# A mixture-of-experts stage with five weight sets, and its down product in 32-row blocks on four column tiles

## The chip, the cores and the metric

The kernel runs on one core of a Trainium2 chip. The metric is the device time of one execution in microseconds (us), lower is better. Before the change it is 932.44 us, the median of three runs (931.26 to 933.4).

## The reference, cut to what matters

One streaming step of a one-layer encoder for 512 prompt tokens and 64 sample tokens (576 in all, width 1024, fp32): a combined projection, an SSD and an S5 mixer, cross-attention over 256 memory rows, a two-level mixture of experts, and a final norm. The change is in the experts. Each token takes two of 32 experts, and every expert's weights are read, 3 MiB for each:

```python
for e in range(N_EXPERTS):                                       # 32
    hid = jax.nn.silu(t @ p["w_gate"][e]) * (t @ p["w_up"][e])   # (T,1024) @ (1024,256), twice
    out = out + (hid @ p["w_down"][e]) * combine[:, e:e + 1]     # (T,256) @ (256,1024)
```

## The kernel before, in words

The kernel is written out by hand, engine by engine, with semaphores. The dense part (projections, mixers, attention) runs until the routing is known. It streams its weights through a ring of six 1 MiB slots. After it comes the expert stage, which is this case.

**One expert.** Routing gives each expert a list of up to 80 rows (`CAP`). For expert n, GpSimd (POOL) issues an indirect DMA that gathers the rows from DRAM (`gather`, L802, into `xg[b]`). TensorE turns them in eight transposes (`turn_x`, recorded under L865, into banks 0 and 1). ScalarE and VectorE copy the turned rows to `xgT[b]` (L1695, L2244). TensorE computes gate and up (L1375: 64 fp32 matmuls of 80 columns on two column tiles of 64; the trace shows each fp32 matmul as two instructions, each with a weight load, so 128). ScalarE takes the silu (L1700), and VectorE multiplies (recorded under L1755, into `hid[b]`). TensorE computes down (L1387: four fp32 matmuls, 80 rows by 512 columns, eight instructions in the trace). ScalarE and VectorE copy one half each to `yo[b]` (L1707, L2257), and POOL scatters the rows to DRAM with a second indirect DMA (`scatter`, L817).

**Buffers.** `xg`, `xgT`, `gact`, `hid`, `yo` and the banks of down (4 and 5, or 6 and 7) exist twice; b is the parity of n, so experts take them in turn.

**Order on TensorE.** gate/up of n, transposes of n+1, down of n, gate/up of n+1. The transposes lie between gate/up and down, so that silu and product run meanwhile. **Order on POOL.** scatter of n, gather of n+3. A gather waits until the expert that used its `xg` buffer last has been turned. A scatter, and the copies to `yo` before it, wait until the last scatter from the same buffer has landed.

**Weights.** Four sets of three 1 MiB parts (gate, up, down), `WSET`. SyncE (SP) loads expert n+4 into the set of n: gate and up when gate/up of n is done, down when down of n is done (`load_part`, recorded under L654). The first four sets are loaded during the last of the dense part, each part when its memory is free (`WFREE`). TensorE's loop has four experts in its body, the loops of the other engines two; the first and last experts are written out. `pass` loops for more than 80 rows per expert exist and are skipped here.

L991 is another product of the dense part: a weight block of 8 columns against 128 columns, with its four token tiles at output partitions 0, 32, 64 and 96, that is on four column tiles, 64 instructions in rounds of four.

Of the kernel before, what the change touches and what calls it, by code (L numbers as in the profile page):

```python
# [12 lines left out]
ACT = mybir.ActivationFunctionType  # L13
# [6 lines left out]
D = 1024  # L20
# [19 lines left out]
CW = 256  # L40
# [5 lines left out]
CAP = 80  # L46
PASSES = -(-T // CAP)
SKIP = float(1 << 12)
# [172 lines left out]
def build(nc, a, o):  # L221
# [14 lines left out]
    with ExitStack() as ctx:  # L236
# [179 lines left out]
        more_loaded = [sem(f"more_loaded{i}") for i in range(6)]  # L416
# [44 lines left out]
        xg_zero, experts_done = sem("gather_buffers_zeroed"), sem("experts_done")  # L461

# [40 lines left out]
        def wait_chunk(eng, c):  # L503
# [12 lines left out]
        LAST = NE // 2 - 1  # L516
# [5 lines left out]
        WSET = [ring_k[0:3], ring_k[3:6], [g0, g1, a0], [a1, b0, b1]]  # L522
        WSEM = [ring_loaded[0:3], ring_loaded[3:6], more_loaded[0:3], more_loaded[3:6]]
        SETS = len(WSET)
        QUADS = NE // SETS

        WFREE = ([chunk_end[max(c for c in range(NCH) if c % SLOTS == k)] for k in range(SLOTS)]
                 + [("pv", 2 * NT - 1)] * 2 + [("route", NT - 1)] * 2 + [("o", NT - 1, 1)] * 2)
        WDENSE = [len(range(i, NCH, SLOTS)) for i in range(SLOTS)] + [0] * 6
# [4 lines left out]
        def wait_expert_chunk(eng, part, qq, s):  # L534

            eng.wait_ge(WSEM[s][part], 16 * qq + 16 * (WDENSE[3 * s + part] + 1))

# [14 lines left out]
        def _(sp):  # L552
# [91 lines left out]
            def load_part(qq, i, s, part):  # L644

                if isinstance(qq, int) and qq == 0:
                    wait_filled(sp, *WFREE[3 * s + part])
                    if s == 2:
                        sp.wait_ge(kv_stored, 32)
                elif part < 2:  # L650
                    sp.wait_ge(gu_done, 4 * qq + (s - 3))
                else:
                    sp.wait_ge(dn_done, 8 * qq + (2 * s - 6))
                sp.dma_start(WSET[s][part], experts_of[part][bass.ds(SETS * i + s, 1), :, :]  # L654
                             .rearrange("e p n -> p (e n)")).then_inc(WSEM[s][part], 16)

            def sp_pass(p):
                first = p * QUADS

                order = [(0, 0), (1, 2), (2, 0), (2, 1), (0, 1), (0, 2), (1, 0), (1, 1), (2, 2), (3, 0), (3, 1), (3, 2)]  # L660
                for s, part in (order if isinstance(p, int) else sorted(order)):
                    load_part(first, 0, s, part)
# [1693 lines left out]
```

## Time and profile before

| what | value |
|---|---|
| median of three runs | 932.44 us (931.26 to 933.4) |
| the profiled execution | 939.89 us, its span 938.1 us |
| TensorE busy | 857.6 us (91% of the span) |
| mean granted TensorE clock | 0.96 of 2.4 GHz |
| expert stage: first gate/up to last down | 598.1 to 899.8 us of the span |
| memory traffic | 166.5 MB, of which 100.7 MB are expert weights |

The span runs from the first instruction to the last; the profiled execution adds 1.8 us around it. Engines are PE (TensorE matmul), PEld (its weight loads), DVE (VectorE), ACT (ScalarE), POOL (GpSimd) and SP (SyncE, which only issues DMAs). "L1387" is a line of the kernel. Matmuls are pipelined, so a row's mean duration is longer than the distance from one to the next; the distance is what counts in a sum.

### The profile page before, as it was taken

To read this page: it belongs to the slowest core of one execution; us is meant where nothing else is said; L and a number is where in the kernel's file an instruction comes from. 1 tells how busy PE (TensorE), PEld (TensorE's weight loads), DVE (VectorE), ACT (ScalarE), POOL (GpSimd) and SP (SyncE) were. 2 spreads that over 40 slices of the span, in tenths; PEclk is the share of its full clock that TensorE was granted. 3 is DMA by queue.
4 is the path that set the end of the run, shared out by engine and by line. 5 is a ranking of instruction groups with operands and counts; after the bars stand their busy time and mean duration, and the time that the engine had idled before them with its cause. 6 is when DMAs were issued, how large, how long until landed. Compare 5 with 4: busy or idle time off the path is not lost. (4 is left out here: it accounts for less than half of the span.)

```text
span 938.1 us, 18956 instructions
## 1 busy us (share of the span) xinstructions
PE 857.6 (91%) x7993; PEld 679.9 (72%) x7993; DVE 354.7 (38%) x767; ACT 195.4 (21%) x435; POOL 144.3 (15%) x175
## 2 busy tenths in 40 slices
PE   3999999889999999999999996799999999999930
PEld 2778877777888888877888885676767676767620
DVE  5599896524551123401223448211111111111117
ACT  2312307325221101112221211111111111111104
POOL 1190100003420000000000000121212222222103
PEclk9999999989999999999999997699999999999975
DMA  9630073202121840241020036599999999999435
GB/s 247 206 98 1 10 176 106 74 13 93 46 90 68 292 169 1 70 155 45 1 90 23 23 113 258 195 346 351 360 350 356 361 361 375 370 364 369 147 139 187
DMA packets 71418, 166.48 MB, mean 177 GB/s; under 512 B 20592, under 2 KB 51440, under 8 KB 58496
## 3 DMA queue, kind: packets, MB, share of 16 engines
q1 hardware_dynamic: 58500, 150.86, 45.5%
q0 software_dynamic: 6144, 9.45, 3.0%
q10 hardware_dynamic: 6716, 5.34, 1.8%
q8 instruction: 43, 0.70, 0.3%
q14 instruction: 15, 0.12, 0.0%
HBM read 158.09 MB, written 17.88 MB: 188 GB/s over the span
## 5 line engine op out<-in xcount | busy, mean ns | idle before, releaser
L898 PE MATMUL bank<-act_a,weight_ring 128*128 128x288 f32 x768 | 190.5, 409 | 1.8 <-ACT act_a L1427 1.8
L898 PEld LDWEIGHTS bank<-act_a,weight_ring 128*128 128x128 f32 x768 | 146.1, 191 | 42.0 <-ACT act_a L1427 2.4
L1206 PE MATMUL bank<-weight_ring,act_b 128*128 128x256 f32 x512 | 111.8, 379 | 0.0
L1206 PEld LDWEIGHTS bank<-weight_ring,act_b 128*128 128x128 f32 x512 | 96.7, 190 | 12.9
L1375 PEld LDWEIGHTS bank<-region_t,weight_ring 128*64 128x64 f32 x2048 | 75.4, 142 | 12.9 <-issue 12.0
L1375 PE MATMUL bank<-region_t,weight_ring 128*64 128x80 f32 x2048 | 77.9, 238 | 0.7 <-ACT region_t L1695 0.7
L1755 DVE TENSOR_TENSOR region_t<-region_t,bank 128x160 f32<-128x160 f32 (+3 forms) x47 | 15.6, 331 | 145.7 <-PE bank L1375 145.3
L817 POOL DMA_INDIRECT expert_rows<-region_r,scatter_now x32 | 30.1, 940 | 207.2 <-DVE region_r L2257 207.2
L2257 DVE COPY region_r<-bank 80x512 f32<-80x512 f32 x32 | 22.0, 687 | 103.9 <-PE bank L1387 103.9
L1387 PE MATMUL bank<-weight_ring,region_t 128*80 128x512 f32 x128 | 58.2, 597 | 1.5 <-DVE region_t L1755 1.0
L1110 PE MATMUL bank<-weight_ring,region_u 128*128 128x256 f32 x256 | 58.3, 388 | 0.0
L1110 PEld LDWEIGHTS bank<-weight_ring,region_u 128*128 128x128 f32 x256 | 49.5, 194 | 7.1
L865 PE MATMUL bank<-ident,region_r 80*128 80x80 f32 (+2 forms) x328 | 45.2, 281 | 3.9 <-DMA region_r<-ffn_rows,gather_index 3.9
L1427 ACT ACTIVATE act_a<-bank 128x512 f32<-128x512 f32 (+1 forms) x46 | 22.5, 523 | 120.4 <-PE bank L865 91.5
L1755 DVE TENSOR_TENSOR region_u<-region_u,bank 128x512 f32<-128x512 f32 (+1 forms) x20 | 13.7, 687 | 85.0 <-PE bank L1206 81.5
L865 PEld LDWEIGHTS bank<-ident,region_r 80*128 80x128 f32 (+2 forms) x328 | 39.2, 190 | 8.5 <-issue 4.5
L785 POOL MEMSET region_r<- 80x1024 f32 x2 | 1.8, 948 | 267.8 <-PE bank L1266 267.8
L1375 PEld LDWEIGHTS bank<-region_t,region_g 128*64 128x64 f32 x1024 | 36.5, 138 | 6.4 <-issue 6.4
L865 PE MATMUL bank<-ident,row_stage 128*128 128x128 f32 (+3 forms) x173 | 23.1, 283 | 18.7 <-DVE row_stage L1773 16.8
L1387 PEld LDWEIGHTS bank<-weight_ring,region_t 128*80 128x80 f32 x128 | 17.9, 150 | 29.9 <-issue 29.4
L1375 PE MATMUL bank<-region_t,region_g 128*64 128x80 f32 x1024 | 37.8, 234 | 0.0
L1700 ACT ACTIVATE region_t<-bank 128x160 f32<-128x160 f32 x32 | 9.7, 303 | 133.2 <-PE bank L1375 133.2
(332 smaller groups left out, 1107.3 us busy)
## 6 DMA issues: line engine op xcount, KB each, us to landing
weight_ring<-in_w_gate SPq DMA_DIRECT2D x16, 1024.0 KB
weight_ring<-in_w_down SPq DMA_DIRECT2D x16, 1024.0 KB
weight_ring<-in_w_up SPq DMA_DIRECT2D x16, 1024.0 KB
weight_ring<-in_w_in SPq DMA_DIRECT2D x8, 1024.0 KB
region_g<-in_w_gate SPq DMA_DIRECT2D x8, 1024.0 KB
region_g<-in_w_up SPq DMA_DIRECT2D x8, 1024.0 KB
act_a<-in_w_down SPq DMA_DIRECT2D x8, 1024.0 KB
act_a<-in_w_gate SPq DMA_DIRECT2D x8, 1024.0 KB
```

The costliest lines, as they stand in the source:

```text
L785: pool.memset(xg[b][0:CAP], 0.0).then_inc(xg_zero, 1)
L817: pool.indirect_dma_start(out=y2_dram[:, :], out_offset=bass.IndirectOffsetOnAxis(ap=cur_y[0:CAP, b:b + 1], axis=0), in_=yo[b][0:CAP], in_ ...
L865: return pe.transpose(out, in_, ident[0:m, 0:m])
L898: m = pe.matmul(ps[:, 0:HALF], slot(c)[:, k, P * (mt % 2):P * (mt % 2 + 1)], x[:, k, HALF * h:HALF * (h + 1)], start=(k == 0), stop=(k == ...
L1110: m = pe.matmul(ps[:, 0:CW], mnT[:, k, P * t:P * (t + 1)], slot(first_chunk + c)[:, k, :], start=(k == 0), stop=(k == KD - 1))
L1206: m = pe.matmul(ps[0:L, CW * cc:CW * (cc + 1)], x[:, k, t0:t0 + L], slot(c)[:, k, :], start=(k == 0), stop=(k == KD - 1))
L1375: m = pe.matmul(banks[2 + part][cols, CAP * j:CAP * (j + 1)], w[:, k, j::2][:, cols], xgT[b][:, k, :], start=(k == 0), stop=(k == KD - 1))
L1387: m = pe.matmul(banks[4 + 2 * b + h][0:CAP, :], hid[b][:, j, :], down[:, D * j + 512 * h:D * j + 512 * (h + 1)], start=(j == 0), stop=(j = ...
L1427: act.activation(dst, src, func, scale=scale).then_inc(emptied["act"], 1)
L1700: act.activation(gact[b].rearrange("p j l -> p (j l)"), banks[2][:, 0:2 * CAP], ACT.Silu)\
L1755: return dve.tensor_tensor(out, x, y, op)
L2257: dve.tensor_copy(yo[b][0:CAP, 512:D], banks[5 + 2 * b][0:CAP, :]).then_inc(yo_dve, 1)
```

## The change

Three things are changed together.

1. **Five weight sets.** `SETS = 5`; the three extra parts lie in memory that the dense part has left by then (`conv_io`, the upper half of `region_t`), and all parts are grouped anew by the time at which their memory is free. Fifteen loads are issued ahead (`PREFETCH`); SP loads expert n+5 into the set of n.
2. **Down in blocks.** The 80 rows are cut into blocks of 32, 32 and 16, the 1024 columns into quarters of 256. The twelve (block, quarter) pairs run in three rounds of four, each round on the four column tiles: blocks 0, 1, 2 of quarter r, and block r of quarter 3. An expert's down is 24 fp32 matmuls of 256 columns. ScalarE makes three copies from the banks where it made one, VectorE two where it made one.
3. **Loops of five.** All engines write out seven experts and then loop five times over five. The double buffers follow `side(n) = n % 5 % 2`: 0, 1, 0, 1, 0, and again 0, 1, 0, 1, 0. The experts 4 and 5, 9 and 10, and so on to 29 and 30 take the same buffer in direct succession (six pairs).

The order of the steps on TensorE is unchanged, and so is POOL's order (scatter n, gather n+3). The core of the diff:

```diff
+DB = 32
+SETS = 5
+PEEL = 2 + SETS
+ROUNDS = (NE - PEEL) // SETS
...
+        def down_block(b, blk, quarter):
+            p0 = DB * 3 if quarter == 3 else DB * blk
+            spot = blk if quarter == 3 else quarter
+            n_ = min(CAP, DB * (blk + 1)) - DB * blk
+            return banks[4 + 2 * b + spot // 2][p0:p0 + n_, CW * (spot % 2):CW * (spot % 2 + 1)]
...
-        WSET = [ring_k[0:3], ring_k[3:6], [g0, g1, a0], [a1, b0, b1]]
+        c0, c1, t1 = view(conv, 0, 2048), view(conv, 2048, 2048), view(reg_t, 2048, 2048)
+        WSET = [[t1, ring_k[5], ring_k[0]], [c0, g0, c1], [g1, ring_k[1], ring_k[2]],
+                [ring_k[3], ring_k[4], b0], [b1, a0, a1]]
+        PREFETCH = [(0, 1), (0, 2), (1, 1), (2, 0), (0, 0), (1, 0), (1, 2), (2, 1), (2, 2), (3, 0), (3, 1), (3, 2),
+                    (4, 0), (4, 1), (4, 2)]
...
+        def side(n):
+            return n % SETS % 2
...
+        def wait_rows_free(eng, n, i, p):
+            done = times_used(n, i, p) - 1
+            if not isinstance(done, int) or done > 0:
+                eng.wait_ge(scattered[side(n)], 16 * done)
...
+            def reload(p, i, n):                                   # SyncE
+                N = NE * p + SETS * i + n
+                for part in range(3):
+                    if part < 2:
+                        sp.wait_ge(gu_done, N - (SETS - 1))
+                    else:
+                        sp.wait_ge(dn_done, 2 * N - 2 * (SETS - 1))
+                    load_part(SETS * i + n, n % SETS, part)
...
+            def gather(n, i, p, reused=True):                      # GpSimd
+                b = side(n)
                 if reused:
-                    pool.wait_ge(turned_x, 4 * pp + (2 * b - 2))
+                    before_it = max(m for m in range(-SETS, n) if side(m) == b)
+                    pool.wait_ge(turned_x, 2 * NE * p + 2 * SETS * i + 2 * (before_it + 1))
...
-                for h in range(2):                                 # TensorE, down
-                    for j in range(2):
-                        m = pe.matmul(banks[4 + 2 * b + h][0:CAP, :], hid[b][:, j, :],
-                                      down[:, D * j + 512 * h:D * j + 512 * (h + 1)], start=(j == 0), stop=(j == 1))
-                    m.then_inc(dn_done, 1)
+                for r in range(3):
+                    for j in range(2):
+                        for blk, quarter in [(0, r), (1, r), (2, r), (r, 3)]:
+                            m = pe.matmul(down_block(b, blk, quarter), hid[b][:, j, DB * blk:min(CAP, DB * (blk + 1))],
+                                          down[:, D * j + CW * quarter:D * j + CW * (quarter + 1)],
+                                          start=(j == 0), stop=(j == 1))
+                    if r > 0:
+                        m.then_inc(dn_done, 1)
...
+                with pe.Fori(0, ROUNDS) as i:
+                    for n in range(PEEL, PEEL + SETS):
+                        turn_x(n, i, p)
+                        down_rows(n - 1, i, p)
+                        gate_up(n, i, p)
+                down_rows(NE - 1, 0, p)
...
+                wait_rows_free(act, n, i, p)                       # ScalarE
+                for blk in range(2):
+                    act.activation(yo[b][DB * blk:DB * (blk + 1), 3 * CW:D], down_block(b, blk, 3), ACT.Copy)
                 act.activation(yo[b][0:CAP, 0:512], banks[4 + 2 * b][0:CAP, :], ACT.Copy).then_inc(yo_act, 1)
...
-                dve.tensor_copy(yo[b][0:CAP, 512:D], banks[5 + 2 * b][0:CAP, :]).then_inc(yo_dve, 1)
+                dve.tensor_copy(yo[b][DB * 2:CAP, 3 * CW:D], down_block(b, 2, 3))
+                dve.tensor_copy(yo[b][0:CAP, 2 * CW:3 * CW], banks[5 + 2 * b][0:CAP, 0:CW]).then_inc(yo_dve, 1)
```

## Rows read from the trace of the kernel before

**Rows 1.** The page: busy time by engine, then 40 slices of the span.

```profile
PE 857.6 (91%) x7993; PEld 679.9 (72%) x7993; DVE 354.7 (38%) x767; ACT 195.4 (21%) x435; POOL 144.3 (15%) x175
...
PEclk9999999989999999999999997699999999999975
DMA  9630073202121840241020036599999999999435
```

**Rows 2.** Busy time in one window of the expert stage.

```profile
core 0: us, PE busy (x) PEld busy (x) DVE busy (x) ACT busy (x) POOL busy (x), PEclk, DMA share, GB/s
672.00:866.00 194.00, 192.45 (x2967) 136.49 (x2967) 30.69 (x61) 27.24 (x61) 47.25 (x82) 1.00 0.98 363
```

**Rows 3.** Waits of TensorE, 620 to 900 us, its only row: sum, times, longest.

```profile
PE bank L1387 <- DVE region_t L1755: 1.5, 6, 0.5
```

**Rows 4.** Timeline, one expert of the steady stretch, weight loads left out.

```profile
703.54 0.69 DVE L2257 COPY region_r<-bank 80x512 f32<-80x512 f32 x1 [3.33 <-PE bank L1387]
705.21 0.94 POOL L817 DMA_INDIRECT expert_rows<-region_r,scatter_now  x1 [6.35 <-DVE region_r L2257]
...
707.21 0.98 POOL L802 DMA_INDIRECT region_r<-ffn_rows,gather_now  x1 [0.86 <-POOL gather_now L796]
...
707.92 1.11 PE L865 MATMUL bank<-ident,region_r 80*128 80x80 f32 x8
...
709.05 3.66 PE L1387 MATMUL bank<-act_b,region_t 128*80 128x512 f32 x8
...
711.03 0.59 ACT L1707 ACTIVATE region_r<-bank 80x512 f32<-80x512 f32 x1 [1.93 <-PE bank L1387]
...
712.64 4.83 PE L1375 MATMUL bank<-region_t,weight_ring 128*64 128x80 f32 x128
...
717.41 1.11 PE L865 MATMUL bank<-ident,region_r 80*128 80x80 f32 x8
...
718.12 0.44 ACT L1695 ACTIVATE region_t<-bank 128x320 f32<-128x320 f32 x1 [1.96 <-PE bank L865]
```

**Rows 5.** Matmul groups by form: count, then busy us, mean ns, idle before.

```profile
L1387 PE MATMUL bank<-weight_ring,region_t 128*80 128x512 f32 x128 | 58.2, 597 | 1.5 <-DVE region_t L1755 1.0
...
L991 PE MATMUL bank<-act_a,w_dt 128*8 128x128 f32 x64 | 2.1, 273 | 0.0
```

**Rows 6.** Timeline, the first expert and the first reused gather.

```profile
591.99 1.20 POOL L802 DMA_INDIRECT region_r<-ffn_rows,gather_index  x1 [44.45 <-issue]
...
596.12 1.30 PE L865 MATMUL bank<-ident,region_r 80*128 80x80 f32 x8 [3.89 <-DMA region_r<-ffn_rows,gather_index]
...
597.60 0.18 POOL L796 COPY gather_now<-gather_index 80x1 int32<-80x1 int32 x1 [3.15 <-PE bank L865]
...
598.12 6.96 PE L1375 MATMUL bank<-region_t,weight_ring 128*64 128x80 f32 x128 [0.70 <-ACT region_t L1695]
598.65 0.97 POOL L802 DMA_INDIRECT region_r<-ffn_rows,gather_now  x1 [0.87 <-POOL gather_now L796]
```

**Rows 7.** Timeline of SyncE, first reload of a weight set.

```profile
605.26 0.35 SPq L654 DMA_DIRECT2D weight_ring<-in_w_gate  x1
```

**Rows 8.** The scatter line, the whole run: issue to landing.

```profile
DMA to landing us min/median/max: 3.3/7.5/7.8
```

**Rows 9.** DMA queue of gathers and scatters, 672 to 866 us: packets, MB, share.

```profile
q0 software_dynamic: 3940, 6.59, 9.8%
```

**Rows 10.** The page: the queue that fetches instructions, whole run.

```profile
q8 instruction: 43, 0.70, 0.3%
```

**Rows 11.** Windows around a short lull of TensorE: busy, clock (PEclk).

```profile
200.00:203.60 3.60, 1.89 (x16) 1.50 (x15) 2.40 (x4) 1.96 (x3) 0.00 (x0) 1.00 0.25 73
203.00:207.00 4.00, 4.00 (x11) 2.89 (x10) 0.00 (x0) 0.41 (x1) 0.00 (x0) 0.58 0.00 0
```

**Rows 12.** Timeline of TensorE there.

```profile
200.82 0.70 PE L865 MATMUL bank<-ident,region_u 72*128 72x72 f32 x8 [0.60 <-ACT region_u L1427]
202.63 5.57 PE L1048 MATMUL bank<-act_b,weight_ring 128*128 128x288 f32 x15 [1.12 <-DVE act_b L1758]
```

More of the change, by code:

```diff
@@ L657, in sp_pass, with load_part @@
[L657 to L662, printed above, removed]
-                with sp.Fori(1, QUADS) as i:
+            def load_part(e, s, part):
+                sp.dma_start(WSET[s][part], experts_of[part][bass.ds(e, 1), :, :]
+                             .rearrange("e p n -> p (e n)")).then_inc(WSEM[s][part], 16)
@@ L664, in sp_pass @@
                     for s in range(SETS):
                         for part in range(3):
-                            load_part(first + i, i, s, part)
+                            load_part(s, s, part)
+                whole = NE // SETS - 1
+                with sp.Fori(0, whole) as i:
+                    for s in range(SETS):
+                        reload(p, i, SETS + s)
+                for n in range(SETS * (whole + 1), NE):
+                    reload(p, 0, n)
             sp_pass(0)
@@ L1707, in act_expert @@
                 act.activation(yo[b][0:CAP, 0:512], banks[4 + 2 * b][0:CAP, :], ACT.Copy).then_inc(yo_act, 1)
             def act_pass(p):
-                first = p * (LAST + 1)
-                again = not isinstance(p, int)
-                copy_x(first, 0)
-                for b in range(2):
-                    act_expert(first, b, reused=again)
-                with act.Fori(1, LAST) as i:
-                    for b in range(2):
-                        act_expert(first + i, b)
-                for b in range(2):
-                    act_expert(first + LAST, b, last=(b == 1))
+                copy_x(0, 0, p)
@@ L1721, in _ @@
+                act_gate(0, 0, p)
+                for n in range(1, PEEL):
+                    copy_x(n, 0, p)
+                    act_rows(n - 1, 0, p)
+                    act_gate(n, 0, p)
+                with act.Fori(0, ROUNDS) as i:
+                    for n in range(PEEL, PEEL + SETS):
+                        copy_x(n, i, p)
+                        act_rows(n - 1, i, p)
+                        act_gate(n, i, p)
+                act_rows(NE - 1, 0, p)
             act_pass(0)
@@ L2300, in dve_pass @@
                     expert_gates()
[L2301 to L2308 removed]
+                copy_x(0, 0, p)
+                dve_hidden(0, 0, p)
+                for n in range(1, PEEL):
+                    copy_x(n, 0, p)
+                    dve_rows(n - 1, 0, p)
+                    dve_hidden(n, 0, p)
+                with dve.Fori(0, ROUNDS) as i:
+                    for n in range(PEEL, PEEL + SETS):
+                        copy_x(n, i, p)
+                        dve_rows(n - 1, i, p)
+                        dve_hidden(n, i, p)
+                dve_rows(NE - 1, 0, p)
             dve_pass(0)
```

195 lines of the change are left out of this document (94 added, 101 removed).

## The prediction

> **What bounds the kernel now.** I read the page first, then windows, the waits of TensorE, the timeline of one expert, and the DMA queues. TensorE is busy 91% of the span [rows 1]. In the last third, the expert stage, two digits stand side by side: from the 27th slice to the 37th the TensorE clock and the DMA row both show 9 in every slice. So both could be the bound. The window from 672 to 866 us tells them apart: TensorE is busy 192.45 of 194 us, the DMA engines 98%, at 363 GB/s [rows 2]. An expert has 144 matmul instructions (128 for gate/up, 8 transposes, 8 for down), so 2967 of them are 20.6 experts, one per 9.42 us. If the weights were late, TensorE would show idle time ahead of L1375. Its only waits from 620 to 900 us are 1.5 us, and on VectorE's product [rows 3]. TensorE sets the pace, and the DMA engines stand just beside the limit.
>
> The timeline shows what the 9.42 us are: transposes 707.92 to 709.05 (1.13), down 709.05 to 712.64 (3.59), gate/up 712.64 to 717.41 (4.77 here; 4.70 is what the mean leaves) [rows 4]. Whatever TensorE sheds per expert counts 32 times, until something else is late. Behind it stand the gather, whose rows are turned next, and the weights.
>
> **Down in blocks.** Before: eight instructions of 512 columns, 58.2 us for 128 [rows 5], so near 0.43 us from one to the next by the length of L1387 in the timeline; 8 x 0.43 = 3.44, and 3.59 to the next line's start leaves 0.15 of hand-over. A pass is thus 0.84 ns per column. After: 48 instructions of 256 columns, 0.215 us each. One after the other they would take 10.3 us, so all hangs on four running at once. L991 is the trace's own case of four column tiles with all 128 rows: 64 instructions of 128 columns, 0.107 us each, 6.8 us in a row, yet 2.1 us busy [rows 5]. Less the last one's 0.27, that is 0.122 us for each round of four. The upper bound for down is 12 rounds x 0.215 x 0.122 / 0.107 = 2.94 plus 0.15, so 3.09 us; the lower 12 x 0.215 + 0.15 = 2.73. I take 2.75, near the lower end, as the excess of L991 is partly its start and would weigh half as much on rounds twice as long. The saving is 0.84 us per expert (bounds 0.50 to 0.86), x 32 = **26.9 us** (16 to 27.5).
>
> The Trainium skill, page "TensorE: Matmul & The Clock Gate", section "Measured speedup vs the span model", gives 2.38 times for three column tiles, 79% of full overlap. By it a down would be 2.58 / 0.79 + 0.15 = 3.4 us and the saving 6 us in all. L991 shows at least 88%, and by it the sum above stands.
>
> The copies: ScalarE needs 0.44 us for 320 columns and 0.59 for 512 [rows 4], so 0.39 for 256; two more make 0.8 us, and it may start at two thirds of down. VectorE's 0.69 becomes two copies, about 0.85. Both lie beside gate/up of the next expert (4.7 us); the scatter is issued 0.2 us later. Cost on the path: 0.
>
> **The fifth set.** Per expert the DMA engines move 3.15 MB of weights and 6.59 / 20.6 = 0.32 MB of rows [rows 9]; at 363 GB/s that is 9.55 us, more than TensorE's new pace of 8.6. They would fall behind by about 1 us per expert, and prefetch pays for it. The first reload goes out at 605.26 [rows 7]. After the change 27 experts are still to come: 605 + 27 x 9.55 = 863 us, with latency 867. TensorE wants the last set, by the sum below, at about 884 (598.1 + 2.3 of cold clock + 31 x 9.42 - 26 + 18). Hidden with 17 us to spare; cost and gain 0. Were no stall to come, it would want it at 866, so the weights would cap the gain at about 25. The three more loads ahead fall in the dense part, where the DMA row has slices of 0 and 2 [rows 1]; SP's two added waits are for stores long done, and behind them SP has only these loads.
>
> **Loops of five, uneven turn.** This is the step that costs. Let expert 4 and 5 share a buffer. The gather of 5 may go only when 4 has been turned; before, it went when 3 had been. Queued behind that wait on POOL are the scatter of 3 and the gather of 6, both with time to spare. From the end of the transposes of 4: POOL reacts after 0.18 (597.42 to 597.60), copies its index and issues after 1.05 (598.65) [rows 6], the gather lands, 0.1 to TensorE. Meanwhile TensorE does down of 3 and gate/up of 4, 2.75 + 4.70 = 7.45 us, and stands. How long a gather takes no row says. From below, the first one is 591.99 to 596.12, 4.1 us, on quieter queues [rows 6]. From above, the one of 707.21 had landed without a wait at 717.41, 10.2 us [rows 4]. The nearest row is the scatter of the same 80 rows: 7.5 us median, 7.8 at most [rows 8]. I take 8.0. Then each stall is 0.18 + 1.05 + 8.0 + 0.1 - 7.45 = 1.9 us, and six pairs make **+11.4 us**.
>
> A second wait hangs on the same pair: the copies to `yo` of expert 5 wait for the scatter of 4. From the end of down of 4: copies and scatter issue 0.1 + 0.85 + 0.98 = 1.9 (0.98 as from 704.23, the copy's end, to 705.21 [rows 4]), landed at 9.5. Down of 5 ends at 8.6, so its copies end at 10.9, its scatter goes at 11.9, the gather of 8 at 13.9, landed 21.9; TensorE wants it at 21.9. Regularly it lands 1.3 us early. I price it 0.3 us at five places, **+1.5**.
>
> The clock: a stall and the transposes after it are 3 us in which TensorE does next to nothing. The trace has a like place: idle 0.60 and 1.12 around 0.70 of transposes [rows 12], and then a clock of 0.58 in the window of 203 to 207 [rows 11], that is some 3.4 us at 1.2 GHz, half of them lost, 1.7 us. It is the only such place that I lean on, so I charge three of the six stalls: **+5.1** (0 to 10).
>
> **Sum.** -26.9 + 11.4 + 1.5 + 5.1 = -8.9 us, on the profiled execution 939.9 to 931.0. The median of the runs lies 7.5 us below that execution; the difference is in neither term, so I predict 932.44 - 8.9 = **923.5 us**.
>
> **The rivals.**
> (a) The uneven turn costs nothing: if a gather lands in 6.1 us or less it is hidden. For: the lower bound of 4.1. Against: the scatters' 7.5. Time: -25, 907.
> (b) The loop does not stay in the instruction memory. TensorE's loop body grows from 4 x 288 to 5 x 368 = 1840 matmuls and loads. The 43 instruction fetches took 0.3% of 16 engines' 938 us, 1.05 us each [rows 10]; gathers and scatters slow down by 7.5 / 3.3 = 2.3 beside the weights [rows 8], so a backward jump that must fetch costs 1.05 to 2.4. Four jumps: +4.2 to +9.6, 928 to 933. For: nothing in the trace had so long a body. Against: 1152 fetched nothing visible. The Trainium skill, page "Runtime: NRT & Kernel Launch", section "Instruction fetch mechanics", gives TensorE 2048 instructions in blocks of 256 and warns of a taken branch to a block not held. By that page's figure 1840 and the waits fit only barely; no run here shows it yet.
> (c) Slower: gathers take longer than before because TensorE's faster pace fills the DMA engines wholly. Each us on a gather costs 6 for the pairs and 5 for the ripples, 11 us, so it decides from 8.0 + 8.9 / 11 = 8.8 us. At 9.5 it is 940, at the bound of 10.2 about 948. For: the share is 0.98 already. Against: it was 0.98 when scatters took 7.5.
> (d) The four blocks overlap only in part: down 3.1 to 3.4 us, saving 6 to 16, stalls 1.3 to 1.6 each, clock +5: 930 to 939.
>
> **How the numbers follow.** The forecast has 0.50, its own range 916 to 930. (a) 0.13, (b) 0.14, (c) 0.14, (d) 0.09. A change under 0.2% (930.6 to 934.3) is about what a measurement of this kernel can't tell from none. Faster: 0.49 + 0.13 + 0.06 of (b) + 0.02 = 0.70. Same: 0.01 + 0.06 of (b) + 0.02 of (c) + 0.03 of (d) = 0.12. Slower: 0.18. The range 911 to 937 leaves out most of (a) and the upper part of (c), 0.2 together.
>
> **What would show it.** Down: distance from its first instruction to the next line's, 2.75 us. Stalls: TensorE idle ahead of L865's transposes of experts 5, 10, ..., 30, released by a gather, near 1.9 us, none of that size elsewhere; PEclk below 1 after some. (b): idle of TensorE's queue after experts 11, 16, 21, 26. Weights: no idle ahead of the gate matmuls. I am wrong if down is over 3.1 us, if stalls of the pairs are under 1 or over 2.7 us, or if TensorE waits at other experts.

## The result and the profile after

The changed kernel takes 965.62 us (median of 4 runs, 963.13 to 968.57), the kernel before, beside it on the same chip, 931.85 us (4 runs, 931.17 to 933.4). The ratio is 1.0365, 95% interval 1.0342 to 1.0389: 33.8 us slower. The forecast was 923.5 us, with a range up to 937. The profiled execution of after took 963.13 us, with a span of 961.3 us. The expert stage runs from 599.9 to 923.3 us, 323.4 us; it was 301.7 us in the profiled execution of before.

The page of after: TensorE's busy time, the clock and DMA rows in 40 slices, and the queue that fetches instructions.

```profile
PE 845.2 (88%) x9273; PEld 695.6 (72%) x9273; DVE 359.8 (37%) x799; ACT 219.5 (23%) x499; POOL 144.1 (15%) x175
...
PEclk9999999989999999999999995999989999898975
DMA  9630073102212920510111528799989979898135
...
q8 instruction: 82, 1.34, 0.6%
```

Two things stand out against [rows 1] and [rows 10]. The DMA row no longer shows 9 in every slice of the stage, so the memory side isn't full: both former bounds now have slack at the same time. And the instruction queue brought 82 blocks where it had brought 43. Next, the window of [rows 2] in after, then the waits of TensorE in the stretch of [rows 3] (sum, times, longest).

```profile
672.00:866.00 194.00, 164.34 (x3331) 128.96 (x3324) 29.92 (x72) 37.96 (x91) 41.50 (x72) 0.92 0.89 325
```

```profile
PE bank L915 <- issue: 19.7, 4, 5.5
PE bank L915 <- DMA region_r<-ffn_rows,gather_now: 10.1, 5, 3.5
PE bank L1426 <- issue: 8.1, 8, 1.7
```

"issue" is time in which TensorE waited for nothing that the profile shows. Four such waits, near 5 us each, stand ahead of the transposes (L915) of experts 12, 17, 22 and 27: these are the four backward jumps of the loop. Eight more lie within gate/up (L1426), three of them, 3.0 us, ahead of the first jump. The gathers account for five waits at the experts with the shared buffer, as forecast (the sixth, ahead of expert 30, has none), and there is none on weights. One jump in the timeline of TensorE:

```profile
705.02 2.38 PE L1426 MATMUL bank<-region_t,region_g 128*64 128x80 f32 x64
712.50 1.32 PE L915 MATMUL bank<-ident,region_r 80*128 80x80 f32 x8 [5.10 <-issue]
713.76 4.56 PE L1442 MATMUL bank<-conv_io,region_t 128*32 128x256 f32 x48
718.24 2.44 PE L1426 MATMUL bank<-region_t,region_g 128*64 128x80 f32 x64
```

The gap is 5.10 us, and the down after it takes 4.56 us where an undisturbed one takes 2.80. The windows say why: the granted clock fell within the gap and stayed at half (0.50, that is 1.2 of 2.4 GHz) for the down behind it.

```profile
710.50:717.30 6.80, 4.80 (x44) 2.89 (x48) 0.49 (x1) 0.44 (x1) 0.00 (x0) 0.50 0.83 337
765.20:772.00 6.80, 6.22 (x56) 3.35 (x56) 0.49 (x1) 1.57 (x4) 0.00 (x0) 0.50 0.58 235
```

Seven such stretches, 3.4 or 6.8 us long and 37.4 us in all, lie between 690 and 882 us.

### The profile page after: what moved, and what is told of

It is laid out like the page before. It is cut to its first block and busy times, and to the rows that moved or that the text cites. A ratio compares the mean times of both kernels' runs of the same rounds, so it can differ in the third digit from the quotient of the medians.

```text
span 961.3 us, 21505 instructions
## 1 busy us (share of the span) xinstructions
PE 845.2 (88%) x9273; PEld 695.6 (72%) x9273; DVE 359.8 (37%) x799; ACT 219.5 (23%) x499; POOL 144.1 (15%) x175
## 5 line engine op out<-in xcount | busy, mean ns | idle before, releaser
L948 PE MATMUL bank<-act_a,weight_ring 128*128 128x288 f32 x768 | 193.0, 413 | 1.8 <-ACT act_a L1487 1.8
L1256 PEld LDWEIGHTS bank<-weight_ring,act_b 128*128 128x128 f32 x512 | 97.0, 190 | 12.7
L915 PE MATMUL bank<-ident,region_r 80*128 80x80 f32 (+2 forms) x328 | 46.1, 287 | 33.3 <-issue 19.7
L915 PEld LDWEIGHTS bank<-ident,region_r 80*128 80x128 f32 (+2 forms) x328 | 39.7, 192 | 38.5 <-issue 24.5
L1426 PE MATMUL bank<-region_t,weight_ring 128*64 128x80 f32 x1600 | 60.4, 234 | 4.7 <-issue 4.7
L1426 PEld LDWEIGHTS bank<-region_t,weight_ring 128*64 128x64 f32 x1600 | 57.5, 140 | 8.1 <-issue 8.1
L2326 DVE COPY region_r<-bank 16x256 f32<-16x256 f32 x32 | 13.7, 429 | 89.9 <-PE bank L1442 83.8
L1770 ACT ACTIVATE region_r<-bank 32x256 f32<-32x256 f32 x64 | 24.2, 378 | 81.3 <-PE bank L1442 69.4
L1755 ACT ACTIVATE region_t<-bank 128x320 f32<-128x320 f32 x32 | 14.0, 437 | 120.3 <-PE bank L915 120.3
L915 PE MATMUL bank<-ident,row_stage 128*128 128x128 f32 (+3 forms) x173 | 23.1, 283 | 19.1 <-DVE row_stage L1839 17.0
L1487 ACT ACTIVATE act_b<-bank 128x288 f32<-128x288 f32 x32 | 12.9, 410 | 103.3 <-PE bank L948 95.7
L1442 PE MATMUL bank<-weight_ring,region_t 128*32 128x256 f32 (+1 forms) x624 | 36.4, 381 | 0.0
L2310 DVE COPY region_t<-bank 128x320 f32<-128x320 f32 x32 | 15.7, 492 | 54.6 <-PE bank L915 54.6
```

What stands on the lines that cost most here:

```text
L915: return pe.transpose(out, in_, ident[0:m, 0:m])
L948: m = pe.matmul(ps[:, 0:HALF], slot(c)[:, k, P * (mt % 2):P * (mt % 2 + 1)], x[:, k, HALF * h:HALF * (h + 1)], start=(k == 0), stop=(k == ...
L1256: m = pe.matmul(ps[0:L, CW * cc:CW * (cc + 1)], x[:, k, t0:t0 + L], slot(c)[:, k, :], start=(k == 0), stop=(k == KD - 1))
L1426: m = pe.matmul(banks[2 + part][cols, CAP * j:CAP * (j + 1)], w[:, k, j::2][:, cols], xgT[b][:, k, :], start=(k == 0), stop=(k == KD - 1))
L1442: m = pe.matmul(down_block(b, blk, quarter), hid[b][:, j, DB * blk:min(CAP, DB * (blk + 1))], down[:, D * j + CW * quarter:D * j + CW * (q ...
L1487: act.activation(dst, src, func, scale=scale).then_inc(emptied["act"], 1)
```

## The experiments

Ratios are against the kernel before on the same chip, with their 95% intervals, whose median was 931.7 to 932.7 us in each group. "Held" means that a loop's instructions stay in TensorE's instruction memory from turn to turn; the count of the instruction queue shows it. Where a kernel was executed only once, no interval can be given and the text says so.

### First group: which of the three parts costs

**TensorE's loop written out** (a_pe_straight), everything else as in after:

```diff
-                with pe.Fori(0, ROUNDS) as i:
-                    for n in range(PEEL, PEEL + SETS):
-                        turn_x(n, i, p)
...
+                if not again:
+                    for n in range(PEEL, NE):
+                        turn_x(n, 0, p)
...
```

> The changed kernel with one edit: TensorE's loop over five experts is written out, so its stream has no backward jump; all other engines keep their loops, the uneven turn stays. Theory 1 (code: TensorE's loop body of some 1,875 instructions is not held, so each backward jump waits for instruction fetches): the four stalls after experts 11, 16, 21 and 26 (19.7 us together) and about half of the stretches at half clock go, 965 becomes about 936; the short halts inside gate/up may stay, as the stream is fetched once in any case. Theory 2 (uneven turn): the gather stalls of the pairs stay, 10 us or more, and nothing else goes. Theory 3 (five sets crowd the DMA queues, and the long stalls are late transfers): the time stays near 965.

Measured: 932.61 us (926.36 to 935.44), ratio 1.0008 (0.9983 to 1.0032). The same work in straight code is 33.0 us faster than in the loop, and that is as much as the change lost. TensorE's waits:

```profile
PE bank L915 <- DMA region_r<-ffn_rows,gather_now: 8.8, 7, 3.0
PE bank L1426 <- issue: 4.7, 8, 1.0
PE bank L915 <- issue: 1.3, 2, 0.8
```

The gathers cost nearly what they did; the jumps' 19.7 us have gone.

**After with the old down** (a_old_down): four fp32 matmuls of 512 columns and one copy each on ScalarE and VectorE, so that the loop body is 1,475 instructions in place of 1,875 (counted in the traces between two branches).

```diff
-                for r in range(3):
-                    for j in range(2):
-                        for blk, quarter in [(0, r), (1, r), (2, r), (r, 3)]:
+                for h in range(2):
+                    for j in range(2):
+                        m = pe.matmul(banks[4 + 2 * b + h][0:CAP, :], hid[b][:, j, :],
+                                      down[:, D * j + 512 * h:D * j + 512 * (h + 1)], start=(j == 0), stop=(j == 1))
...
```

> The changed kernel with the down product of before (eight instructions of 512 columns, two copies to the row buffer), so the loop body shrinks from some 1,875 to some 1,475 instructions; five sets and uneven turn stay. Theory 1 (code): if the limit lies above 1,475, no stall at the backward jumps and none inside gate/up; down costs 27 us more again, the pairs' stalls shrink to about 1.1 us each: 938 to 942. Theory 3 (five sets crowd the DMA queues): the long stalls stay, 980 or more.

Measured: 935.79 us (931.7 to 939.28), ratio 1.0039 (1.0018 to 1.0059). The instruction queue shows 43 blocks, no wait on "issue", and 4.1 us of waits on gathers. The loop is held, and the time lies 2 us under the expected 938 to 942. The rest of the change, uneven turn and fifth set, costs about 4 us at the old pace.

**The kernel before with the new down alone** (b_new_down), four sets, loops of four (1,499 instructions), even turn:

> The kernel before with the new down product alone (32-row blocks on four column tiles, with its copies): four sets, even turn, loop body of four experts, some 1,500 instructions. Theory 1: if 1,500 instructions are held, down saves 0.8 us per expert and nothing takes it back but perhaps the weights near the end: 907 to 913. If they are not held: long stalls at five backward jumps, 935 or more. Theory 2 plays no part. A theory that the blocks themselves cost (copies, tile switches) says 925 or more without any stall at the jumps.

Measured: 921.38 us (920.89 to 921.92), ratio 0.9884 (0.9863 to 0.9905). It is faster, but misses the expected 907 to 913. The waits name the reason, in the columns of [rows 3]:

```profile
PE bank L1383 <- DMA weight_ring<-in_w_up: 4.3, 4, 1.3
PE bank L1383 <- DMA act_b<-in_w_up: 2.2, 2, 1.5
PE bank L1383 <- DMA region_g<-in_w_up: 1.9, 2, 1.4
PE bank L1383 <- issue: 1.7, 2, 1.2
```

Until 795 us an expert takes 8.35 us; then eight gate/ups in a row wait halfway for the up weights and take 5.4 to 6.4 us in place of 4.65. TensorE has caught up with the DMA engines, 8.4 us of waits in all. The timeline shows the new pace and the length of down:

```profile
703.31 4.65 PE L1383 MATMUL bank<-region_t,weight_ring 128*64 128x80 f32 x128
707.89 1.11 PE L873 MATMUL bank<-ident,region_r 80*128 80x80 f32 x8
708.94 2.80 PE L1396 MATMUL bank<-weight_ring,region_t 128*32 128x256 f32 x48
711.66 4.65 PE L1383 MATMUL bank<-region_t,weight_ring 128*64 128x80 f32 x128
```

711.66 - 703.31 = 8.35 us. The same view of a_old_down, where a gate/up is printed in two halves by the memory of its weights, so that an expert runs from 702.28 to 711.34, 9.06 us:

```profile
702.28 2.44 PE L1426 MATMUL bank<-region_t,conv_io 128*64 128x80 f32 x64
...
707.82 3.60 PE L1441 MATMUL bank<-conv_io,region_t 128*80 128x512 f32 x8
711.34 2.44 PE L1426 MATMUL bank<-region_t,region_g 128*64 128x80 f32 x64
```

**The kernel before with a loop of eight experts on TensorE** (b_loop8): the long body (2,356 instructions) without any other part of the change.

```diff
-                with pe.Fori(1, QUADS - 1) as i:
-                    for s in range(SETS):
-                        expert(first + i, s)
+                with pe.Fori(0, (QUADS - 2) // 2) as i:
+                    for q in range(2):
+                        for s in range(SETS):
+                            expert(first + 2 * i + (1 + q), s)
```

> The kernel before with one edit: TensorE's loop has eight experts in its body in place of four (some 2,380 instructions in place of 1,190), three rounds instead of six. Same instructions in the same order. Theory 1 (code): two backward jumps that must fetch, 5 us each, with some half-clock stretches behind them: 942 to 952. Theories 2 and 3: 932, no change.

Measured: 943.43 us (941.63 to 944.83), ratio 1.0112 (1.0088 to 1.0136); 67 blocks, and these waits of TensorE:

```profile
PE bank L1375 <- issue: 7.7, 6, 3.3
```

So a long body alone makes the kernel 11 us slower, with two backward jumps only. The two jumps account for waits of 2.5 and 3.3 us, less than in after, though the trace has the two branch instructions with 6.0 and 6.8 us. The jump comes here behind a down of 512 columns: the first branch begins at 708.09, and TensorE is busy with that down until 711.97.

The traces have the same record for every backward jump, the branch of TensorE. It lasts 0.21 to 0.25 us in all kernels whose count says "held" (before, a_old_down, b_new_down and those that follow), and 3.5 to 6.8 us in all others; in after 5.7, 4.8, 6.0 and 5.6 us.

### Second group: what the turn of the buffers costs, and whether the place of the loop matters

**Even turn, all loops written out** (c_even), and **the same with the old down** (c_even_old):

```diff
-PEEL = 2 + SETS
+PEEL = NE
...
-            return n % SETS % 2
+            return n % 2
```

> The changed kernel with the buffers in strict turn, n % 2, which needs the expert loops of all engines written out; five sets and the down in blocks stay. Theory: with TensorE's loop written out, what is left of the loss is the uneven turn: 8.8 us of waits on gathers at six places, and half-clock stretches after some of them. Both go, so the stage is paced by TensorE at 8.6 us per expert, or by the weights: 912 to 921 us, no wait of TensorE on a gather, none on weights, fetch halts of 5 us or less as with TensorE alone written out. Rival 1 (TensorE's rate is not the bound any more, the DMA engines are): 919 to 925, and the gather waits come back at other experts or turn into waits for the up weights late in the stage. Rival 2 (the fetches of the written-out code, at a rate of one per 256 instructions, cost what the turn gave): 928 to 933.

> The same, with the down of before (four matmuls of 512 columns): five sets, even turn, all loops written out. Against the changed kernel with the old down (uneven turn, loops, 935.8) it has no wait on gathers, 4.1 us there, and against the kernel before it has the fifth set and straight code. Theory: at TensorE's old pace (9.42 us per expert) nothing is late, so 932, no change against before: the fifth set is worth nothing there and straight code costs nothing. Rival (fetching while the DMA engines are 98% busy costs by itself): 935 to 940 with halts of TensorE within gate/up.

Measured: c_even 931.65 us (924.38 to 936.41), ratio 0.9993 (0.9972 to 1.0014); c_even_old 936.8 us (934.82 to 938.61), ratio 1.005 (1.0033 to 1.0067). Both theories failed, and the times are those of the rivals that priced the fetching of straight code (928 to 933 and 935 to 940). In c_even the waits on gathers are gone, and TensorE waits for its instructions instead:

```profile
PE bank L1421 <- issue: 9.5, 9, 1.7
PE bank L910 <- issue: 1.8, 2, 1.1
PE bank L1437 <- issue: 1.8, 2, 1.4
```

13.1 us here, against 8.8 + 4.7 + 1.3 = 14.8 in a_pe_straight. In straight code fetching is itself a limit. c_even fetched 75 blocks for 18,861 recorded instructions, near 256 for each. At the new pace an expert is 375 instructions in 8.35 us, so a block of 256 lasts 5.7 us, and in gate/up, which has 256 of them, 4.65 us; at the jumps of after TensorE stood for 4.9. At the old pace, 295 instructions in 9.06 us, a block lasts 7.9 us, and c_even_old halts for 1.8 us in all. It is argued from this, not shown, that the fetches caught up during the waits on gathers and became the limit without them. Of the 4.1 us that c_even_old loses on before, the halts explain less than half; the rest stays open.

**The start of after's loop shifted by 84 and 170 instructions** (c_pad84, c_pad170):

```diff
             pe.wait_ge(ident_ready, 1)
+            for _ in range(42):                    # 85 in the other
+                pe.transpose(banks[7][0:8, 0:8], ident[0:8, 0:8], ident[0:8, 0:8])
```

> The changed kernel with 42 transposes of 8 x 8 (84 instructions) put at the start of TensorE's program, which only shifts where its loop of 1,875 instructions lies in memory. The question is why the body is fetched anew each turn. If it is the place (1,875 instructions touch eight blocks of 256 or nine, by where they begin), one of the two shifts of 84 and 170 brings the loop to eight blocks, the fetch queue falls from 82 packets to about 45, and the time to 935 or less. If a body of this size is never held (the block beyond its end is fetched as well), both stay at 80 packets or more and at 960 to 970 us.

> As for the shift of 84, with 85 transposes (170 instructions). By the place: at least one of the two at about 45 packets and 935 us or less. By the size: 80 packets or more and 960 to 970 us.

Measured, one execution each: 959.72 and 971.52 us, 83 blocks fetched in both. A body of 1,875 isn't held at any of the three places. The place still changes the price. Shifted by 84, TensorE waits 4.1 to 4.4 us at a jump; shifted by 170, 3.1 to 4.6 us, but 3.2 to 3.7 us more within the down behind it.

### Third group: a version that uses what was found, and the price of a fetch by itself

**Straight code in place of the held loop** (e_4straight): b_new_down with TensorE's loop written out for the first pass.

> The kernel before with the new down alone, and TensorE's loop of four experts written out for the first pass: the same work on every engine, with straight code in place of a held loop. Theory: a block of 256 instructions lasts 6.0 us at the new pace (368 in 8.6 us) and 4.65 within gate/up, no longer than a fetch takes beside the weight streams, so TensorE halts in gate/up as in the written-out kernels with five sets (9 to 13 us of halts, then half-clock stretches): 928 to 934 against 921.4. Rival (straight code is free, and the written-out kernels with five sets lost to something else): 920 to 923.

Measured: 931.08 us (928.66 to 934.23), ratio 0.9993 (0.9974 to 1.0011), so 9.7 us slower than the held loop (the ratios, 0.9993 against 0.9884, say the same), with 11.8 us of "issue" waits within gate/up. The rival is refuted; straight code isn't free here. The Trainium skill, page "Runtime: NRT & Kernel Launch", section "Instruction fetch mechanics", says that crossing a block is mostly hidden and that kernels prefer full unrolling; beside full DMA queues and small matmuls this run shows the opposite.

**Reloads of an eighth** (e_noload): after, with each reload reduced to 16 partitions. It leaves out most of the weights from expert 5 on.

```diff
-                    load_part(SETS * i + n, n % SETS, part)
+                    load_part(SETS * i + n, n % SETS, part, 16)
```

> The changed kernel, but each reload brings only 16 of the 128 partitions of a weight part, so from expert 5 on the weights are mostly those of the first five experts (that part of the computation is left out); TensorE's program, its loop of 1,875 instructions and the uneven turn stay. It tells what a fetch costs by itself from what it costs beside the weight streams. Theory: the price of a backward jump and of the halts is the time that a 16 KB fetch waits in queues that are 98% busy, so the four jumps fall from 5.0 us each to 1.0 to 2.4, the halts within gate/up and the waits on gathers go, the fetch queue still shows about 80 packets, and the time is 905 to 918. Rival (the price is the sequencer's own): four jumps of 4 to 5.5 us remain, 925 to 935.

Measured, one execution: 929.29 us, 82 blocks. The waits of TensorE, 620 to 900 us, and the window of [rows 2], with a DMA share of 0.36 in place of after's 0.89:

```profile
PE bank L915 <- issue: 12.6, 4, 3.4
PE bank L1426 <- issue: 1.3, 1, 1.3
```

```profile
672.00:866.00 194.00, 180.05 (x3773) 143.85 (x3774) 34.74 (x84) 43.63 (x104) 47.48 (x83) 0.96 0.36 79
```

The time is the rival's (925 to 935), but the price of a jump lies between the two: of 4.9 us, 12.6 / 4 = 3.15 remain on light queues, and the weight streams add 1.8. The trace's list of packets shows the difference: in after two blocks arrive within each gap before TensorE goes on, in e_noload one. The 4.9 us belong to this place of the loop; beside full queues a jump costs 3.8 us on average in c_pad170 and 5.6 in e_mix3 (below). The halts within gate/up (8.1 us, now 1.3) and the waits on gathers (10.1 us, now none) came with the full queues.

**New down for three of five experts** (e_mix3), body 1,715:

```diff
+BLOCKED = (0, 2, 3)                        # n % 5 with the new down; the others have the old one
...
+                if n % SETS not in BLOCKED:
```

> The changed kernel with the down in blocks for three of every five experts (n % 5 = 0, 2, 3) and the old down for two: TensorE's loop body is about 1,715 instructions, between 1,500 (held) and 1,875 (not held). If 1,715 is held, the fetch queue stays near 45 to 50 packets, no jump costs anything, and the time is 925 to 932 (three fifths of the gain of down, less the uneven turn's waits). If it is not held, 80 packets less a few, four jumps of 4 to 5 us and 945 to 960.

Measured: 970.13 us (966.97 to 972.5), ratio 1.0412 (1.038 to 1.0445), 81 blocks, 22.2 us of waits at four jumps. Not held, and 10 us over the 945 to 960 expected for that.

**The spare set for expert 4** (d_once): new down, loops of four, even turn; set 4 holds expert 4's weights, the other four go round.

```diff
...
+            return n if n < HELD else (n - HELD) % SETS           # set_of(n), HELD = 5, SETS = 4
```

> The down in blocks with loops of four experts and the even turn, and the fifth weight set used once only: it holds the weights of expert 4, loaded ahead; from expert 5 on the four other sets go round. TensorE's loop body is four experts, about 1,500 instructions, as in the kernel before with the new down alone (921.4), which was held. Theory: that kernel lost its last 10 us because the weights fell behind from expert 23 on; one set more of prefetch is 3 MB, 8.6 us of DMA time. So 911 to 915 us, no halts at jumps, no wait on gathers over 0.5 us, waits on up weights only in the last experts or none. Rival (the DMA engines' rate over the whole stage sets the end, and loading ahead only moves the bytes): 919 to 922. Rival (the new placing of the weight sets costs in the dense part): 918 or more, with the first gate/up later than 600 us.

Measured: 921.21 us (920.08 to 922.79), ratio 0.9888 (0.9867 to 0.9909), nothing gained on b_new_down. The rival had the time right, but not the reason. The windows of d_once show an idle stretch of the DMA engines:

```profile
630.00:640.00 10.00, 9.88 (x229) 8.23 (x226) 1.66 (x4) 2.25 (x6) 3.09 (x7) 1.00 0.97 372
640.00:650.00 10.00, 10.00 (x214) 8.39 (x208) 1.98 (x5) 2.39 (x6) 3.18 (x6) 1.00 0.34 130
650.00:660.00 10.00, 10.00 (x214) 7.88 (x216) 2.15 (x5) 2.24 (x6) 2.31 (x4) 1.00 0.94 352
```

The reload for expert 8 goes when expert 3 is done, the next one only after expert 5. With nothing to load at a share of 0.34, the 3 MB ahead were given back.

### Fourth group

**The spare set for expert 24** (f_late), everything else as in d_once, so that the 3 MB lie ready where the weights fell behind:

```diff
...
+            return SETS if n == SPARE else (n - (n > SPARE)) % SETS   # set_of(n), SPARE = 24
```

> Down in blocks, loops of four, even turn, and the fifth set used once, but for expert 24 and not for expert 4: loaded ahead, it lies there until the time at which the weights fell behind in the kernel before with the new down (from expert 23). With the spare set on expert 4 the DMA engines had nothing to load between the reloads for experts 8 and 9, so the bytes loaded ahead were lost again as idle DMA time. Theory: here the DMA engines stay fed, and the 3 MB loaded ahead (8.6 us) take away the waits for up weights: 911 to 915 us, waits on up weights under 3 us in all, DMA share 0.97 or more from 640 to 840 us. Rival (the loading ahead in the dense part only delays something else, or the extra straight code costs its gain): 918 to 922.

Measured: 916.65 us (914.08 to 919.9), ratio 0.984 (0.9815 to 0.9865). It is the fastest kernel of the study, 15.0 us below before. The time lies between the theory's 911 to 915 and the rival's 918 to 922; the two signs of the theory, short waits on weights and a full DMA row, came. The DMA engines were busy 0.99 of 640 to 840 us:

```profile
640.00:840.00 200.00, 196.90 (x4305) 160.63 (x4304) 39.32 (x95) 49.77 (x119) 53.22 (x92) 1.00 0.99 376
```

```profile
PE bank L1441 <- issue: 2.2, 3, 1.3
PE bank L930 <- issue: 1.5, 1, 1.5
PE bank L1441 <- DMA weight_ring<-in_w_up: 1.4, 2, 1.2
```

Waits on weights are 1.4 us where b_new_down had 8.4. The first two rows are halts for instructions, 2.0 us more of them than in b_new_down; this kernel has eight experts written out after the loop.

**f_late with the buffers in the turn 0, 1, 1, 0** (f_pairs), 15 pairs of experts on one buffer in a loop that is held:

```diff
-            return n % SETS % 2
+            return (0, 1, 1, 0)[n % SETS]
```

> The kernel with the spare set for expert 24, with the buffers in the turn 0, 1, 1, 0: every second expert follows one that used the same buffer, 15 pairs from expert 2 on in place of none. It prices the uneven turn alone, in a loop that is held, beside the new down. By the prediction a pair stalls TensorE 1.9 us, with 1.7 us for the clock after half of them: 15 x 1.9 + 7 x 1.7 = 40 us slower than the even turn at most, less what the weights would have cost; 940 to 955. Rival (the queues are less full once TensorE waits, so a gather lands in less than 7 us and most of it is hidden): under 10 us slower, 915 to 925.

Measured: 954.1 us (949.77 to 958.49), ratio 1.0233 (1.0193 to 1.0273), 37.5 us slower than f_late, 2.5 us per pair. The whole stage has 25.2 us of waits on gathers at 14 places, of which in 620 to 905 us:

```profile
PE bank L930 <- DMA region_r<-ffn_rows,gather_now: 23.7, 13, 2.7
```

25.2 / 14 = 1.8 us each. After ten of them (waits of 1.2 to 2.7 us) the down took 4.0 to 4.5 us in place of 2.8, as here; after the four others (1.4 to 2.0 us) it did not.

```profile
716.68 1.11 PE L930 MATMUL bank<-ident,region_r 80*128 80x80 f32 x8 [2.72 <-DMA region_r<-ffn_rows,gather_now]
717.72 4.47 PE L1457 MATMUL bank<-act_b,region_t 128*32 128x256 f32 x48
```

**How long a body is held**: the new down for one and for two of five experts (f_mix1, f_mix2), and e_mix3 shifted by 84 and 170 instructions (g_mix3_pad84, g_mix3_pad170).

> The changed kernel with the down in blocks for one of five experts (n % 5 = 2) and the old one for four: TensorE's loop body is about 1,555 instructions, between 1,475 and 1,500 (held) and 1,715 (not held). If the eight blocks of 256 must hold the body and a block fetched ahead, the border lies between 1,537 and 1,792 by where the body begins: held is somewhat likelier, about 45 fetches and 930 to 935 us. Not held: about 80 fetches, four jumps of 5 to 6 us, 960 to 970 us.

> As before, with the down in blocks for two of five experts (n % 5 = 0, 2): a body of about 1,635 instructions. Held: about 45 fetches, 927 to 933 us. Not held (somewhat likelier): about 80 fetches, 960 to 970 us.

> The kernel with the down in blocks for three of five experts, whose loop body of 1,715 instructions was fetched anew each turn (970.1), with 84 instructions put at the start of TensorE's program, so that the body begins elsewhere within a block of 256. Theory (the place decides: the body must lie in seven blocks, as the next block is fetched too): 1,635 was held, 1,715 lies in seven blocks only if it begins in the first 77 of one, and one of the two shifts of 84 and 170 is likely to bring it there: about 45 fetches, no jump stalls, 925 to 935 us. Rival (the size alone decides, the border is between 1,635 and 1,715): about 80 fetches and 960 to 975 us at both shifts.

> As for the shift of 84, with a shift of 170 instructions. By the place: likely one of the two is held (about 45 fetches, 925 to 935 us). By the size: both at about 80 fetches and 960 to 975 us.

| kernel | body | blocks fetched | time, us |
|---|---|---|---|
| a_old_down | 1,475 | 43 | 935.8 |
| b_new_down | 1,499 | 46 | 921.4 |
| f_mix1 | 1,555 | 43 | 938.1 (one execution) |
| f_mix2 | 1,635 | 44 | 928.3 (one execution) |
| e_mix3 | 1,715 | 81 | 970.1 |
| e_mix3 shifted by 84 | 1,715 | 81 | 971.0 (one execution) |
| e_mix3 shifted by 170 | 1,715 | 45 | 930.5 (one execution) |
| after, three places | 1,875 | 82, 83, 83 | 965.6, 959.7, 971.5 (the last two one execution each) |
| b_loop8 | 2,356 | 67 (three turns of the loop) | 943.4 |

f_mix1 is held, yet its 938.1 us lie over the expected 930 to 935; that stays open. The same body of 1,715 instructions is held or isn't, by where it begins: 170 idle instructions at the very start of the program make the kernel 40 us faster. The two pages' rows of the instruction queue, shifted by 84 and by 170:

```profile
q8 instruction: 81, 1.33, 0.5%
```

```profile
q8 instruction: 45, 0.74, 0.3%
```

This fits a memory of eight blocks of 256 in which the block behind the body needs a place too: 1,715 lies in seven blocks from 78 of 256 starts, 1,875 from none. The packets of the instruction queue bear the last part out. From one turn of the loop to the next nine blocks are fetched (ten in the last one of three of them) in after, c_pad84, c_pad170, e_mix3 and e_mix3 shifted by 84, and none or one in the held kernels. A body of 1,715 can touch at most eight blocks, so the ninth lies behind it. The Trainium skill, page "Runtime: NRT & Kernel Launch", section "Instruction fetch mechanics", gives TensorE 2048 instructions, refilled in blocks of 256, which makes the eight; the table agrees.

## Why the prediction was wrong, step by step

**Down in blocks, -26.9: right in kind, a little too large.** Down takes 2.80 us, 2.72 from its first instruction to the next line's (711.66 - 708.94), for 2.75 forecast, and all four blocks run at once, so rival (d) is out. The saving is 9.06 - 8.35 = 0.71 us per expert, 22.7 in all, not 0.84. The new length was right. The old one, 3.59, was read from an execution 7.5 us above its median, in which an expert took 9.4 us; in a_old_down it is 3.52 (711.34 - 707.82), and b_loop8 has the same 9.06 us per expert without any other part of the change. That leaves 0.80, and of it 0.09 goes where the forecast had nothing: from the transposes to the first instruction of down it is 1.05 us (708.94 - 707.89) in place of 0.96 (707.82 - 706.86).

**The fifth set, cost and gain 0: right here, since TensorE is late itself; wrong about when weights begin to matter.** The prediction let the weights cap the gain at about 25 with five sets. With four sets they cap it much earlier: b_new_down waits 8.4 us for them, f_late 1.4. In after they are never late, since TensorE is.

**The uneven turn, +11.4: right.** After shows 10.1 us in five waits of the six pairs (the last one shows none), from 1.2 to 3.5 us and 2.0 on average; f_pairs has 1.8 us per pair where 1.9 was forecast. The price that no row gave, 8.0 us for a gather, was right too: the median of after's gathers from issue to landing is 7.9 us. The ripple of +1.5 didn't come: no other expert waits on a gather.

**The clock, +5.1: right for the pairs, with luck in the count.** A stall of a pair costs 4.47 - 2.80 = 1.7 us in the down after it, the forecast's figure. In after three of the five stalls are followed by such a down (experts 10, 20 and 25), and three had been charged, but "half" was a guess: in f_pairs it was ten of 14. By this the uneven turn alone is 2.5 us per pair, 15 us for six, against 16.5 for the two terms. What the sum lacked is the four stretches at half clock behind the jumps, which make seven in all.

**The step that failed is rival (b), the loop body.** It was named, with the right place to look, and given a chance of 0.14 and a price of 4.2 to 9.6 us; the sum had it at nothing. The runs show in its place a loss of 33.0 us against straight code. Two things were wrong.
- Its chance. 1,840 "fit only barely" by the figure of 2048; 1,875 counted, and the block behind the body, didn't. None of the three starts tried did, and by the rule above none would.
- Its price. 1.05 us was how long a fetch kept a DMA engine busy, and 2.4 that figure scaled. A fetch does last about that long, but the wait is longer: at the first jump of after the branch stands at 706.66, two blocks come from 707.94 to 708.86 and from 709.98 to 710.91, and TensorE goes on at 712.50. On average it stands for 4.9 us beside the weights, 3.15 with light queues (e_noload). The price was added for four jumps only, where the whole body comes anew each turn, nine blocks: the fetches made eight halts within gate/up, 8.1 us, of which 3.0 us lie ahead of the first jump, and the long gaps halved the clock.

The sum by measured terms: -22.7 (down) + 19.7 (jumps) + 8.1 (halts) + 10.1 (gathers) = +15.2 us. The clock adds 13.5: the seven downs in the stretches at half clock take 12.7 us more than 2.73 us each from line to line, and four groups of transposes 0.2 us more each. That makes +28.7 of the +31.3 by which the profiled execution, 963.13 us, lies above the median of before; 2.6 us stay unexplained. The -22.7 takes it that the median executions of before run at 9.06 us per expert, as b_loop8 does; no trace of one is there to show it. The total of the fetching needs no such sum: the loop against straight code is 33.0 us, and against a held loop, with 170 idle instructions ahead of the 1,715 body, 40.

**Not settled.** Whether a loop of 1,875 could be held with less code in it wasn't tried; the price of straight code was measured with old and new down, but not what sets the time of a single fetch. What a_old_down loses on before, 4 us, looks like the gathers' 4.1 us, but c_even_old has none of them and loses as much, so this isn't settled either. What lets one jump cost 3.8 us and another 5.6 beside the same weight streams is open too.

## What to carry to other kernels

Count a loop body in instructions (an fp32 matmul is four here, with its weight loads) before a change makes the instructions smaller and more numerous, and read the instruction queue's count before and after: 43 blocks against 82 was the verdict here. Here, with full DMA queues and short matmuls, a loop that is just held was worth 9.7 us more than straight code. And a weight set more helps only at the expert where the weights fall behind: the same 3 MB gave nothing at expert 4 and 4.7 us at expert 24 (916.65 against 921.38, with ratios of 0.984 and 0.9884, whose intervals just touch).

## What the runs showed of the hardware

- TensorE's backward branch lasts 0.21 to 0.25 us when its loop is held and 3.5 to 6.8 us when it isn't. It leaves TensorE idle for 3.15 us with the DMA engines 0.36 busy and for 4.9 us with them 0.89 busy (after; 3.8 on average in c_pad170, 5.6 in e_mix3), but for 2.5 and 3.3 us behind a down of 512 columns (b_loop8).
- Bodies up to 1,635 instructions were held at the one place tried, 1,875 at none of three, and 1,715 by its place: 970 us or 930. A body that isn't held is fetched whole in each turn; that one block more comes with it is shown for 1,715, nine blocks a turn where the body touches eight at most.
- Straight code of short matmuls costs 9.7 us over 24 experts against a held loop, by halts of up to 1.8 us.
- Twelve rounds of four concurrent 256-column fp32 matmuls on four column tiles take 2.72 us, 0.227 each, where one alone was put at 0.215.
- After 14 pauses of 1.2 to 2.7 us, each with 1.1 to 1.3 us of transposes behind it, the down that followed took 4.0 to 4.5 us in place of 2.8 ten times and 2.8 four times. The granted clock in one of the ten, from 717.7 to 721.1, was 0.51.
